# Constant matmuls on PE in front of three of the four rows of transpositions

## The reference

```python
h = rms_norm(x, attn_norm_g[l])
proj = h @ w_in[l]
rq, rk, rv, rg, dq, dk, dv = jnp.split(proj, split_at, axis=-1)
...
x = x + jnp.concatenate([ret, da], axis=-1) @ w_out[l]
h = rms_norm(x, ffn_norm_g[l])
x = x + (jax.nn.silu(h @ w_gate[l]) * (h @ w_up[l])) @ w_down[l]
```

```python
h = layer_norm(ALPHA * x + mix @ w_out[l], ln1_g[l], ln1_b[l])
x = layer_norm(ALPHA * h + peer_ffn(h, peer_w_q[l], peer_sub_keys[l], peer_u[l], peer_v[l]),
               ln2_g[l], ln2_b[l])
# peer_ffn, per chunk of 128 tokens:
q = (xc @ w_q).reshape(c, PEER_HEADS, 2, PEER_HALF)
sc = jnp.einsum('chpd,hpnd->chpn', q, sub_keys)
# top 16 of 128 keys, twice; top 16 of the 256 sums; softmax; rows u and v of the table
act = jax.nn.gelu(jnp.einsum('chkd,cd->chk', u_tab[idx], xc), approximate=False)
out = jnp.einsum('chk,chkd->cd', gate * act, v_tab[idx])
```

## Time and profile before

| | |
|---|---|
| time, median of 3 runs | 2427.27 us (2424.07 to 2429.39) |
| the profiled execution's own time | 2430.45 us |
| its span, first to last instruction | 2428.6 us |
| mean granted clock of TensorE | 0.933 |
| PE busy | 2008.6 us (83%), 8464 matmuls |
| DVE busy | 1564.9 us (64%) |
| POOL busy | 1239.6 us (51%) |
| ACT busy | 666.7 us (27%) |
| chain that ended last | PE 39%, DMA 37%, DVE 15%, issue 4% |

### The profile page before, as it was taken

The page is one execution under the profiler, slowest core; times in us unless marked ns, Lnnn a source line. Parts: engine busy times, 40 slices in busy tenths (PEclk is TensorE's granted clock), DMA queues, the critical chain, the costliest instruction groups (busy, mean ns, idle before and its releaser), DMA issues.

```text
span 2428.6 us, 25784 instructions
## 1 busy us (share of the span) xinstructions
PE 2008.6 (83%) x8464; PEld 1324.2 (55%) x8464; DVE 1564.9 (64%) x3650; ACT 666.7 (27%) x1231; POOL 1239.6 (51%) x828
## 2 busy tenths in 40 slices
PE   7989998989999768897777777797688887777776
PEld 6779997779998655443323233276554432322232
DVE  7532116533215658888788877666588987888776
ACT  5524436534435422121101010054321111010100
POOL 7719877728883046565444444140465654444441
PEclk9989999889999778999999999997799999999999
DMA  5415554415545139999999999751399999999996
GB/s 179 159 41 196 186 172 144 156 35 193 196 164 207 61 108 401 420 420 420 421 421 421 421 422 420 298 207 61 114 403 420 421 420 421 421 421 421 421 421 278
DMA packets 118012, 700.21 MB, mean 288 GB/s; under 512 B 13968, under 2 KB 13968, under 8 KB 51856
## 3 DMA queue, kind: packets, MB, share of 16 engines
q0 software_dynamic: 73728, 536.90, 53.4%
q1 hardware_dynamic: 44176, 161.96, 19.0%
HBM read 697.76 MB, written 1.05 MB: 288 GB/s over the span
## 4 chain that ended last, share of the span: by engine, by line
PE 39%; DMA 37%; DVE 15%; issue 4%; ACT 2%; POOL 2%; SPq 0%; DVEq 0%; POOLq 0%; ACTq 0%
PE ps L623 37%; DMA late_row<-in_table,arena 19%; DMA arena<-in_table,arena 17%; DVE arena L2188 2%; DVE diag L2198 2%; DVE late_row L2188 1%; DMA row_sb<-in_table,arena 1%; POOL w_split L1142 1%; DVE arena L1910 1%; ACT arena L1460 1%; DVE arena L1778 1%; ACT w_split L1268 0%; DVE row_sb L2188 0%; POOL arena L1228 0%; DVE arena L1712 0%
## 5 line engine op out<-in xcount | busy, mean ns | idle before, releaser
L1142 POOL TENSOR_TENSOR w_split<-raw,w_split 128x1024 fp32r<-128x1024 f32 x260 | 635.1, 2462 | 423.2 <-ACT w_split L1268 409.5
L623 PE MATMUL ps<-late_row,diag 128*128 128x512 f32 x1000 | 475.4, 620 | 118.0 <-DVE diag L2198 118.0
L623 PE MATMUL ps<-arena,diag 128*128 128x512 f32 x888 | 430.4, 629 | 130.5 <-DVE diag L2198 130.5
L623 PE MATMUL ps<-hT_hi,w_split 128*128 128x256 f32 x2624 | 506.6, 291 | 28.6 <-POOL w_split L1142 24.0
L623 PEld LDWEIGHTS ps<-hT_hi,w_split 128*128 128x128 f32 x2624 | 422.1, 194 | 38.8 <-issue 27.5
L1228 POOL DMA_INDIRECT late_row<-in_table,arena x250 | 284.2, 1137 | 303.3 <-PE ps L623 284.4
L1228 POOL DMA_INDIRECT arena<-in_table,arena x222 | 252.0, 1135 | 320.6 <-PE ps L623 261.9
L623 PEld LDWEIGHTS ps<-late_row,diag 128*128 128x128 f32 x1000 | 187.3, 196 | 396.7 <-DVE diag L2198 203.7
L623 PE MATMUL ps<-hT_lo,w_split 128*128 128x256 f32 x1312 | 375.8, 286 | 0.0
L623 PEld LDWEIGHTS ps<-arena,diag 128*128 128x128 f32 x888 | 167.5, 198 | 375.4 <-DVE diag L2198 205.6
L2188 DVE CUSTOM_DVE_ANT_0 late_row<-late_row,x_res 128x1024 f32<-128x1024 f32 x250 | 307.6, 1235 | 97.3 <-DMA late_row<-in_table,arena 97.3
(11 more groups left out here) (241 smaller groups left out, 1912.5 us busy)
## 6 DMA issues: line engine op xcount, KB each, us to landing
raw<-in_stream SPq DMA_DIRECT2D x288, 512.0 KB, 3.3
row_sb<-in_row SPq DMA_DIRECT2D x2, 2306.5 KB, 11.2
late_row<-in_table,arena POOLq DMA_INDIRECT x250, 30.0
arena<-in_table,arena POOLq DMA_INDIRECT x222, 29.1
arena<-in_sub SPq DMA_DIRECT2D x2, 1024.0 KB, 10.8
arena<-in_small SPq DMA_DIRECT2D x2, 640.0 KB, 8.8
x_res<-in_x SPq DMA_DIRECT2D x1, 1024.0 KB, 5.7
out_x<-x_res SPq DMA_DIRECT2D x2, 512.0 KB, 5.2
```

The costliest lines, as they stand in the source:

```text
L623: ins = nc.tensor.matmul(o, lhsT, rhs, start=start, stop=stop)
L1142: pool.tensor_tensor(w_lo[pair], raw[:, at % raws, :], w_hi[pair].bitcast(F32), ALU.subtract).then_inc(lo_ready, 1)
```

## The change

`transpose_rows` gets a number `turning`. After the banks are open and before the wait for the rows, PE issues that many plain float32 matmuls of `ident` (weights) by `rel` (128x384) into the first bank, each of them starting the bank anew; the transpositions overwrite them. The numbers are 9 for `xT` of block1, 13 for `fT` and 13 for `hT`; `xT` of block2 has none. With two layers of each kind the kernel issues 2 x (9 + 13 + 13) = 70 matmuls more.

```diff
-            def transpose_rows(w, banks, name, src, rows, also=None):
+            def transpose_rows(w, banks, name, src, rows, also=None, turning=0):
 
 
                 bs = [open_bank(pe, banks, f"{name}{i}") for i in range(4)]
+                for _ in range(turning):
+                    nc.tensor.matmul(bs[0][:, 0:3 * P], ident[:], rel[:], start=True, stop=True)
                 for t in range(TT):
                     if rows is not None:
                         pe.wait_ge(rows_ready, rows + t + 1)
...
-                transpose_rows(w, B, "xT", xn, 0)
+                transpose_rows(w, B, "xT", xn, 0, turning=9)
...
-                transpose_rows(w, B, "fT", xn, 2 * TT)
+                transpose_rows(w, B, "fT", xn, 2 * TT, turning=13)
...
-                transpose_rows(w, B, "hT", x_res, 0)
+                transpose_rows(w, B, "hT", x_res, 0, turning=13)
```

## The result

Eleven runs of each kernel on one chip: 2434.66 us after (2430.78 to 2438.33) against 2429.33 before (2423.18 to 2432.27), a ratio of 1.0027 with a 95% interval of 1.0017 to 1.0037. The constants at three turns, meant to keep the clock up there, made the kernel slower by about 6.6 us (0.0027 x 2429; by the interval 4.1 to 9.0, and the two medians are 5.3 apart). The profiled execution took 2438.33, its span is 2436.5 (before: 2430.45 and 2428.6), and the mean granted clock rose from 0.933 to 0.943: the higher clock is there, and the time isn't.

The account below looks back on a forecast made before the run. It took PE's chain to the end to bound the kernel, with all six turns on it. Terms: `fT` +4.0, `hT` -2.9, `xT` +1.3 and +1.2, sum +3.6 us on 2427.27, giving 2431; range 2424.5 to 2438.

Parts of the forecast that it names:

- The price of a matmul: All three places: one added plain f32 matmul costs 0.65 us at full clock, 1.3 at half, and leaves two records.
- Rival D: The constants don't hold the clock; it falls amid the thirteen and transpositions come 6 us late or more: 2455, chance 0.03.
- `fT`: Thirteen last 8.45 us in a hole of 5.4, so hidden blocks start 2.0 us later: +4.0 for two layers.
- `hT`: Thirteen fit before the second half's rows; query chunks run at full clock: -1.45 us each, -2.9 for both layers.
- The step with the weights' high part in front of the banks: At `hT`: ACT's high part waits for the first transpositions, moves to 882.15, and ACT reaches the banks 0.3 us later.
- `xT`, first layer: ACT reaches the banks 2.5 us late, POOL's low parts move with it, less slack of 1.2: +1.3 us.
- the seventh chunk: First layer's `xT`: POOL has this weight chunk ready with 1.2 us slack, so PE gets it 1.3 us later.
- `xT`, second layer: Nine, begun at half clock, end at 376.5; ACT is 2.5 us late against slack of 1.3: +1.2 us.
- The step "PE is let in at about 369.0, with DVE and ACT": Second layer's `xT`: PE can start its constants at about 369.0, when DVE and ACT start working.
- Rival B: At `xT`, the ACT to POOL weights' chain takes over under long low clock: 2435 (3.3 each) to 2441, chance 0.28.
- Rival C: Old kernel's hidden blocks and queries both start at half clock in timed executions, so the change is faster: 2424, chance 0.15.
- The transpositions and the clock: At `fT`, the trace's rise from 0.50 to 1.00 disagrees with the skill's rule; by that rule the sum is -0.2.

Follow-up runs that it names:

- e2: Thirteen constants at `fT` alone, none at `xT` and `hT`, against the kernel before: 2430.14 us, ratio 1.0003 (0.9990 to 1.0016).
- e3: Thirteen constants at `hT` alone, none at `xT` and `fT`, against the kernel before: 2424.5 us, ratio 0.9981 (0.9969 to 0.9992).
- e9: Twenty-six constants at `fT`, none elsewhere, against the kernel before: 2452.4 us against 2434.06, ratio 1.0079 (4 runs).
- e4: Nine constants at `xT` alone, PE's loop over block1's two layers written out, against the kernel before: 2428.92 us, ratio 1.0001.
- e8: As e1, with ACT preparing one more weight chunk ahead of emptying the banks, against the kernel before: 2431.26 us, ratio 1.0008.
- e1: Nine constants at `xT` alone, none at `fT` and `hT`, against the kernel before: 2435.09 us against 2429.36, ratio 1.0029.
- e10: As e5, plus four constants at `xT` behind the transpositions, against the kernel before: 2420.7 us against 2434.06, ratio 0.9958 (7 runs).
- e5: No constants at `xT`, eight at `fT`, ten at `hT`, against the kernel before: 2420.29 us against 2430.2, ratio 0.9969.

## Why the prediction came out as it did

Direction and places were right, and the total was within its range, but low: +3.6 was forecast, +6.6 measured (4.1 to 9.0). That it came so near is in part luck. Timed one at a time, `xT` lost 7.0 where 2.5 was forecast, and `fT` and `hT` together gave 3.9 where a loss of 1.1 was forecast; the two errors cancel in part. Point by point:

- **The price of a matmul.** 0.65 forecast, 0.645 measured in four kernels (8.38 or 8.39 for 13 in after, e2 and e3, 16.77 for 26 in e9), and two records each. Rival D fell: the granted clock stays at 1.00 throughout the thirteen (window 172.9 to 181 in after).
- **`fT`.** +2.0 a layer forecast; 1.86 in the profiles of after and of e2, though only +0.7 for both in e2's time (up to 3.9 by the interval). The hole was measured well, and the transpositions' and ACT's start behind it (1.4 forecast, 182.66 - 181.37 = 1.29 measured).
- **`hT`.** -1.45 a layer forecast, -1.5 in the profiles of after and e3, and -4.6 for both in e3's time (-7.5 to -1.9). The step with the weights' high part in front of the banks held too: ACT's row begins at 893.16 and empties the banks from 894.13.
- **`xT`, first layer: mis-sized.** +1.3 forecast, +2.4 measured at the place and +3.1 up to `fT`. ACT on the banks 2.5 late was forecast and 2.96 measured, since the nine took 7.83 us instead of 7.5; the seventh chunk came 1.66 late (37.70 against 36.04), near the 1.3 forecast. The term failed in looking no further than that chunk: the eighth is 2.4 late, because its raw weights land late, as POOL frees their buffers late. The prediction followed compute from ACT to POOL to PE and left out the fourth link, POOL to the load of the chunk three places on.
- **`xT`, second layer: mis-sized, by a wrong assumption.** +1.2 forecast, +3.6 measured at the place and +4.8 up to `fT`. The step "PE is let in at about 369.0, with DVE and ACT" failed: PE issues 2.30 us after DVE there. 369.0 was where DVE and ACT started, and in the trace of before PE had no row of its own with which to check it, only the wait for the rows. With that, nine at 7.58 us (half clock at first) put ACT at 4.9 late instead of 2.5, on which the chain of the first layer then goes on. e4 shows that the late start goes with the jump of the loop, and e8 that ACT's order sets most of the price in time: with either edit the loss of the nine falls from 7.0 to 0.2 and 1.9 us. Their profiles explain about half of that.
- **Rival B**, at 0.28, was the right mechanism for what came in excess, with its place and its middle price (3.3 each, 2435) close to what was measured, 3.1 and 4.8; only its reason was another. It had the clock staying low for half of the nine or more. They took 7.83 and 7.58 us, where nine at full clock are 5.81, so the lower clock cost 2.0 and 1.8 us, an estimate of 4.0 and 3.5 us at half. PE's late start and the raw buffers made the rest. In another execution it can cost more: in e8's second layer the nine took 8.77 us (373.85 to 382.62). The windows of after in the second layer:
```profile
377.00:380.60 3.60, 3.60 (x7) 1.88 (x6) 3.58 (x3) 1.68 (x2) 2.79 (x1) 0.53 0.05 16
380.90:383.80 2.90, 2.90 (x10) 1.66 (x9) 2.44 (x4) 0.00 (x0) 2.05 (x1) 1.00 0.54 181
```
That is not much longer than the forecast had it. Its 3.2 and 3.4 us stand in no row; the rows had 2.8 at `fT` and 3.7 at `hT`.
- **Rival C**, which had the hidden blocks start at half clock in the timed executions, is seen in two of twelve pieces; e2 leaves room for it.
- **The transpositions and the clock.** In the second layer of e3 and of e8 the hidden blocks started at 0.50, in the ten others at 1.00, with the same transpositions and nothing else ahead of them. So the rule of the Trainium skill, "TensorE: Matmul & The Clock Gate", Part 4, that transposes don't bring the full clock, is contradicted by ten of twelve starts; the two others look as the rule has it. What tells the two apart isn't shown.

What stays open: why PE comes late after the jump (the records have it idle with nothing to wait for; that it is fetching code was only argued), 3 of the 6.2 us between e1 and e4, 2.5 of the 5.1 between e1 and e8, the 3 us between the profile and the timing of e2, and whether e10 beats e5 in time.

## What to carry to other kernels

Work put into a wait to keep the clock up can't be recalled when the wait ends, so size it by the hole at full clock and round down: the same edit was worth +6.6 us with 9, 13 and 13 matmuls and -7.5 with 0, 8 and 10. Before filling a wait that seems free, look at what stands behind it in the other engines' orders as well: in the first `xT` PE's own products started 0.6 us late, and with the chain through ACT, POOL and the raw buffers they were 2.4 late at their end. Check with a row of the engine itself when it is there to start: after a loop's jump it can be later than its neighbours, which a wait hides and a filling lays bare.

## What the runs showed of the hardware

- After the jump of a loop PE issued its first matmul 2.3 us after DVE began on the same signal (376.32 against 374.02; 1.7 and 1.8 in e1 and e8); written out, 0.34 before it (371.52 against 371.86).
- The view of the clock can read 1.00 at the start of the execution while the spacing of the matmuls is that of 0.50: the transpositions of the earlier trace rows took 3.31 us, as the ones at 0.50 do.
- A plain f32 matmul of 128x128 by 128x384 took 0.645 us at a granted clock of 1.00 (8.39 us for 13), and left two records.
- Small rows of DVE last longer while POOL makes a low part of the weights: the row of 128x64 above took 2.34 us in e8, to 19.07, where POOL's third part ended at 19.02, and 0.18 in e1, where POOL was idle.
- The hidden blocks can start at 1.00 or at 0.50 with the same work ahead of them; the piece was 187.35 us long in ten of twelve, 188.77 and 189.23 in the two others.
